# The up-projection of a streaming encoder: all tiles take unnormalised rows, root and shift are applied in PSUM

## The reference

```python
def rms_norm(x, g):
    y = xf * lax.rsqrt(jnp.mean(xf * xf, axis=-1, keepdims=True) + EPS)
    return (y * g)

def conv_ffn(h, w_up, w_conv, b_conv, w_down, prefix):
    up = h @ w_up                                   # 1024 -> 2 * 2816
    ext = jnp.concatenate([prefix, up], axis=1)     # 2 earlier rows
    conv = ext[:, 0:T] * w_conv[0]
    for j in range(1, CONV_W):                      # CONV_W = 3
        conv = conv + ext[:, j:j + T] * w_conv[j]
    conv = conv + b_conv
    gate, val = jnp.split(conv, 2, axis=-1)
    return (jax.nn.silu(gate) * val) @ w_down, ext[:, T:]

    # in a layer, x after the token mixers:
    h = rms_norm(x, g2) * (1 + scale2) + shift2
    f, conv_state = conv_ffn(h, w_up, w_conv, b_conv, w_down, conv_prefix)
    x = x + gate2 * f
```

## Time and profile before

| | us |
|---|---|
| median of 3 runs | 1171.86 |
| lowest and highest of them | 1171.85, 1176.35 |
| the profiled execution, its own time | 1171.43 |
| the span in its trace | 1169.7 |
| what lies around the span | 1.7 |

### The profile page before, as it was taken

How to read it: one execution, slowest core, us unless ns; L and a number is a source line. 1 busy time by engine, 2 the same in 40 slices (tenths; PEclk the granted TensorE clock), 3 DMA queues, 4 the chain that set the end, 5 groups by cost and what they waited for, 6 DMA issues and landing times.

```text
span 1169.7 us, 22931 instructions
## 1 busy us (share of the span) xinstructions
PE 1119.6 (96%) x8368; PEld 1017.8 (87%) x8368; DVE 515.3 (44%) x1297; ACT 591.3 (51%) x1095; POOL 691.8 (59%) x310
## 2 busy tenths in 40 slices
PE   5799999999999899999999999999999999999996
PEld 1687888887889899999998788888889989999996
DVE  0556513546325754442136562355631575444102
ACT  1454444445445666555456544445544566555431
POOL 0454434545455687778778544454556668777782
PEclk8899999999999999999999999999999999999999
DMA  9855546755553355454456555483534325545451
GB/s 361 299 178 207 221 187 237 257 205 195 195 199 111 106 180 170 153 179 158 171 200 237 204 217 197 181 305 119 198 109 140 124 98 180 179 147 177 144 189 71
DMA packets 61821, 215.99 MB, mean 185 GB/s; under 512 B 7896, under 2 KB 8480, under 8 KB 61488
## 3 DMA queue, kind: packets, MB, share of 16 engines
q1 hardware_dynamic: 61744, 214.92, 51.6%
HBM read 209.85 MB, written 5.05 MB: 184 GB/s over the span
## 4 chain that ended last, share of the span: by engine, by line
PE 86%; DVE 6%; POOL 2%; issue 2%; ACT 2%; DMA 1%; SPq 1%; DVEq 0%; POOLq 0%; ACTq 0%
PE ps L637 25%; PE ps L638 23%; PE ps L639 23%; PE ps L590 4%; PE ps L606 2%; POOL wlo L535 1%; PE ps L584 1%; DMA first<-mod_first 1%; POOL hl L553 1%; DVE ps L1758 1%; PE ps L798 1%; DVE merged L1766 1%; PE ps L764 1%; PE ps L674 1%; PE ps L754 1%
## 5 line engine op out<-in xcount | busy, mean ns | idle before, releaser
L535 POOL TENSOR_TENSOR wlo<-raw,whi 128x1024 fp32r<-128x1024 f32 x282 | 673.5, 2392 | 450.4 <-ACT whi L1109 348.2
L637 PE MATMUL ps<-hh,whi 128*128 128x288 f32 (+1 forms) x1648 | 501.4, 304 | 15.2 <-POOL wlo L535 3.6
L638 PE MATMUL ps<-hl,whi 128*128 128x288 f32 (+1 forms) x1648 | 489.6, 297 | 0.0
L639 PE MATMUL ps<-hh,wlo 128*128 128x288 f32 (+1 forms) x1648 | 489.0, 297 | 0.0
L637 PEld LDWEIGHTS ps<-hh,whi 128*128 128x128 f32 x1648 | 312.3, 190 | 55.9 <-issue 37.7
L638 PEld LDWEIGHTS ps<-hl,whi 128*128 128x128 f32 x1648 | 313.1, 190 | 0.6
L639 PEld LDWEIGHTS ps<-hh,wlo 128*128 128x128 f32 x1648 | 312.1, 189 | 0.0
L1109 ACT ACTIVATE whi<-raw 128x1024 fp32r<-128x1024 f32 x204 | 214.6, 1054 | 139.3 <-PE ps L639 108.6
L637 PE MATMUL ps<-fah,whi 128*128 128x290 f32 x352 | 107.4, 305 | 0.0
L638 PE MATMUL ps<-fal,whi 128*128 128x290 f32 x352 | 104.5, 297 | 0.0
L639 PE MATMUL ps<-fah,wlo 128*128 128x290 f32 x352 | 104.4, 297 | 0.0
(11 more groups left out here) (234 smaller groups left out, 1232.4 us busy)
## 6 DMA issues: line engine op xcount, KB each, us to landing
raw<-stream SPq DMA_DIRECT2D x284, 512.0 KB, 4.4
mraw<-stream SPq DMA_DIRECT2D x40, 1024.0 KB
first<-mod_first SPq DMA_DIRECT2D x16, 512.0 KB, 10.7
o_proj<-proj SPq DMA_DIRECT2D x12, 288.0 KB
kvk<-keys_t SPq DMA_DIRECT2D x6, 512.0 KB, 3.8
kvv<-vals SPq DMA_DIRECT2D x6, 512.0 KB, 5.1
cst<-consts SPq DMA_DIRECT2D x1, 1238.0 KB, 17.3
x<-x_fm SPq DMA_DIRECT2D x1, 1152.0 KB, 11.8
```

The costliest lines, as they stand in the source:

```text
L535: nc.gpsimd.tensor_tensor(wlo[:, slot, :], raw[:, slot, :], whi[:, slot, :].bitcast(F32), ALU.subtract).then_inc(lo_ready, 1)
L637: mm(out, whi[:, slot, a:b], high, start=(i == 0 and wcols[2]), stop=False)
L638: mm(out, whi[:, slot, a:b], low, start=False, stop=False)
L639: last = mm(out, wlo[:, slot, a:b], high, start=False, stop=(i == n - 1 and wcols[3]))
```

## The change

All 44 up tiles of a layer now take `oh` and `ol`. `scale_tile` and `shift_up` are applied to each of them, and `up_shifted` takes the place of `piece_done` ahead of the copy of the state. `hup` and everything that made the normalised rows of this stage is gone on DVE, ACT and POOL. PE's tiles 4 and 5, too, now wait for the convolution of tiles 0 and 1 (the loop covers them). The split of piece Q_UP + 4 on ACT is moved ahead of the load of the table for silu, and inside `up_pair` the split of a piece stands ahead of the shift.

```diff
@@ PE
-                for j in range(4):
-                    up_piece(slot_for(l, Q_UP + j), Q_UP + 4 + j, UPB + j, j + 1 if j >= 2 else None, hl_ready if j == 0 else None)
-                with pe.Fori(0, 2 * FT // 4 - 2) as r:
+                with pe.Fori(0, 2 * FT // 4 - 1) as r:
                     for j in range(4):
-                        up_piece(slot_for(l, Q_UP + j), r * 4 + (Q_UP + 8 + j), UPB + j, r * 4 + (j + 5))
+                        pe.wait_ge(lo_ready, upto(l, lo_ready, r * 4 + (Q_UP + 4 + j + 1)))
+                        pe.wait_ge(convolved, upto(l, convolved, r * 4 + (j + 1)))
+                        product(ps[:, UPB + j, 2:2 + CC], slot_for(l, Q_UP + j), (1, 0, True, True), u_terms).then_inc(piece_done, 1)
@@ POOL
-                lows(q, Q_UP + AHEAD)
-                q = lows_and_norm(Q_UP + AHEAD, 2, ((1, 0, 2), (1, 2, 5), (1, 5, KT)))
                 lows(q, NSPLIT + (AHEAD if l + 1 < DEPTH else 0))
@@ ACT
                 high(Q_UP + AHEAD)
                 root(2)
+                high(Q_UP + AHEAD + 1)
                 nc.scalar.preload_act_table_set("silu_and_others")
...
-                for j in range(3):
-                    shift_up(j)
-                    if j < 2:
-                        high(Q_UP + AHEAD + 1 + j)
-                    norm_high(2, *UP_CHUNKS[j])
...
                 def up_pair(p, odd, r=None):
-                    up_tile(p, odd, 0, r)
-                    if r is None and p == 0:
-                        shift_up(3)
+                    next_high(p, odd, 0, r)
+                    shift_up(p, odd, 0)
                     if r is not None or p >= 1:
                         silu(p - 1, 1 - odd)
-                    up_tile(p, odd, 1, r)
+                    up_tile(p, odd, 0, r)
+                    next_high(p, odd, 1, r)
+                    shift_up(p, odd, 1)
                     if r is not None or p >= 1:
                         product_high(p - 1, 1 - odd)
+                    up_tile(p, odd, 1, r)
@@ DVE
-                for j in range(3):
-                    scale_tile(Q_UP + j, up_bank(j), 2, None)
-                    if j == 0:
-                        in_order(V.tensor_copy(ps[:, 7, 0:T], rstd[:]))
-                    normed(2, *UP_CHUNKS[j])
+
+                def scale_up(p, odd, g):
+                    u = 2 * odd + g
+                    dve.wait_ge(piece_done, upto(l, piece_done, p * 2 + (done(Q_UP) + g)))
+                    V.tensor_copy(shifts[:, u, :], ps[:, up_bank(p, u), GAP:GAP + 2])
+                    scale_tile(up_bank(p, u), 2, up_scaled)
...
                 def pair(p, odd, first=False):
-                    convolve(p, odd, 0)
+                    scale_up(p, odd, 0)
                     if not first:
                         multiply(p - 1, 1 - odd)
-                    convolve(p, odd, 1)
+                    convolve(p, odd, 0)
+                    scale_up(p, odd, 1)
                     if not first:
                         product_low(p - 1, 1 - odd)
-
-                convolve(0, 0, 0)
-                scale_tile(Q_UP + 3, up_bank(3), 2, None)
-                convolve(0, 0, 1)
+                    convolve(p, odd, 1)
+
+                pair(0, 0, True)
                 pair(1, 1)
```

More of the change, by code:

```diff
@@ L130 @@
 AHEAD = 3
-NI, NU = 6, 4
+NI = 6
 C_ID, C_ONE = 0, P
@@ L209, in encoder @@
         fal, _, n2 = place("fal", [P, FT, CC], F32R, at=proj_at + n)
-        hup, _, n3 = place("hup", [P, KT, CC], F32, at=proj_at + n + n2)
-        assert n + n2 + n3 <= gates_at + gates_n - proj_at and n + n2 >= proj_n
+        assert n + n2 <= gates_at + gates_n - proj_at
         probs, _, n = place("probs", [P, 1024], F32, at=work_at)
@@ L546, in lows, with norm_low @@
                         low(slot_for(l, q), q)
[L548 to L550 removed]
+                def norm_low(a, b):
                     for k in range(a, b):
[L552 to L553 removed]
+                        pool.wait_ge(hh_ready, upto(l, hh_ready, k + 1))
+                        nc.gpsimd.tensor_tensor(hl[:, k, :], work[:, k, :], hh[:, k, :].bitcast(F32),
                                                 ALU.subtract).then_inc(hl_ready, 1)
[L557 to L564 removed]
                 if l == 0:
@@ L570, in _ @@
                 else:
-                    q = lows_and_norm(Q_IN + AHEAD, 1, ((3, 0, 1), (1, 1, 4), (1, 4, KT)))
-                lows(q, Q_UP + AHEAD)
-                q = lows_and_norm(Q_UP + AHEAD, 2, ((1, 0, 2), (1, 2, 5), (1, 5, KT)))
+                    q = Q_IN + AHEAD
+                    for pieces, a, b in ((3, 0, 1), (1, 1, 4), (1, 4, KT)):
+                        lows(q, q + pieces)
+                        q += pieces
+                        norm_low(a, b)
+                        pool.sem_inc(settled, 1)
                 lows(q, NSPLIT + (AHEAD if l + 1 < DEPTH else 0))
@@ L1031, in _ @@
                         sum_square(l, 2, m - 1)
-                def up_piece(slot, q, bank, convolved_tiles, ready=None):
-                    pe.wait_ge(lo_ready, upto(l, lo_ready, q + 1))
-                    if convolved_tiles is not None:
-                        pe.wait_ge(convolved, upto(l, convolved, convolved_tiles))
-                    product(ps[:, bank, 2:2 + CC], slot, (1, 0, True, True), up_terms, ready, KT).then_inc(piece_done, 1)
-                for j in range(NU):
+                for j in range(4):
                     pe.wait_ge(lo_ready, upto(l, lo_ready, Q_UP + j + 1))
-                    o = ps[:, up_bank(j), 2:2 + CC]
                     if j == 0:
                         pe.wait_ge(pads_ready, upto(l, pads_ready, 1))
+                    o = ps[:, up_bank(j // 2, j), 2:2 + CC]
+                    if j == 0:
                         i = first_tile(o, slot_for(l, Q_UP), 2)
@@ L1548, in in_order, with affine, normed @@
                     dve.wait_ge(dve_own, count[0] + at)
-                def affine(n, k, scaled):
+                def affine(k, scaled):
                     for g, (a, b) in enumerate(((0, TP), (TP, T))):
-                        o = work[:, k, a:b] if n == 1 else hup[:, k, a + 2 * g:b + 2 * g]
-                        i = V.tensor_scalar(o, scaled[:, a:b], norm_a[:, n - 1, k, g:g + 1],
-                                            mod[:, 24 * (n - 1) + k, g:g + 1], ALU.mult, ALU.add)
+                        i = V.tensor_scalar(work[:, k, a:b], scaled[:, a:b], norm_a[:, 0, k, g:g + 1], mod[:, k, g:g + 1],
+                                            ALU.mult, ALU.add)
                     i.then_inc(h_scaled, 1)
-                def normed(n, a, b):
-                    half = [ps[:, bank, 2:2 + T] for bank in (6, 2 if n == 1 else 1)]
-                    at = (n - 1) * KT
+                def normed(a, b):
+                    half = [ps[:, bank, 0:T] for bank in (6, 2)]
                     for k in range(a, b + 1):
@@ L1611, in _ @@
                         dve.wait_ge(x_scaled, upto(l, x_scaled, k + 1))
-                        affine(1, k, work[:, k, :])
+                        affine(k, work[:, k, :])
                         if k:
@@ L1620, in _ @@
                     for t in range(NI):
-                        scale_tile(t, t % 2, 0, cst[:, C_QS + t:C_QS + t + 1])
+                        dve.wait_ge(piece_done, upto(l, piece_done, done(t)))
+                        V.tensor_scalar(shifts[:, t, :], ps[:, t % 2, TP:TP + 2], cst[:, C_QS + t:C_QS + t + 1], None, ALU.mult)
+                        scale_tile(t % 2, 0, in_scaled)
                         if t == 0:
                             in_order(V.tensor_copy(ps[:, 7, 0:T], rstd[:]))
-                        normed(1, *IN_CHUNKS[t])
+                        normed(*IN_CHUNKS[t])
                 def rotate(n):
```

90 lines of the change are left out of this document (34 added, 56 removed).

## The result

| | before | changed |
|---|---|---|
| median of 4 runs each, us | 1173.17 | 1259.48 |
| lowest and highest, us | 1171.85, 1176.35 | 1257.11, 1262.44 |
| the profiled execution, us | 1171.43 | 1257.11 |
| its span, us | 1169.7 | 1255.0 |

The changed kernel takes 1.0733 times as long, with a 95% interval of 1.0695 to 1.0770. The forecast was 1254.5 us, range 1238 to 1275.

What follows compares the result with a forecast made beforehand. The prediction took the turns of DVE and ACT as the bound: 2.61 + 1.69 = 4.30 us a tile against PE's 3.22. That added 2 x 41.4 = 82.8 us to 1171.43, forecast 1254.5 us, range 1238 to 1275.

Steps and rivals of the forecast that it cites:

- What bounds the kernel: Up-stage loop: DVE and ACT work in turns, 2.61 us from state copy to state copy, under PE's 3.22 us tile.
- Removal: Transition into the up stage: dropping normalised rows saves at most 5.2 us a layer, 10.4 us in all, if PE stays bound.
- The turn, 4.30 us: Up-stage loop: 2.61 us plus 1.69 us for scaling, shift, silu or product_high, hand-overs and register steps, against PE's 3.22 us.
- the register step: Loop, between some waits and their instruction: adds 0.08 us a turn on average, with 0 and 0.2 us as ends.
- The start: Layer 0's up stage: first scaling at 387.25 as before, first shift at 388.7, tile 4 scaled at 402.0.
- What comes back: End of the up stage: last tap to last product shortens by 0.3 us; down stage moves by 41.4 us a layer.
- The split: ACT, behind the tail: splitting a weight piece costs nothing, with 0.9 us of cover before the next shift.
- what would show it: Timeline signs: state copies 4.2 to 4.4 us apart, PE idle about 1 us before each up tile, chain over DVE and ACT.
- PE stays the bound: Rival, up loop: scaling and shift overlap the previous tile's convolution, turn under 3.22 us; 1161 us, chance 0.06.
- Silu off the path: Rival, up loop: silu and product_high stay outside the turn, 3.88 us a turn; 1221 us, chance 0.03.
- PE's clock: Rival, up loop: waits lower PE's granted clock until PE is the bound; above 1275 us, chance 0.05.

Runs made afterwards that it cites:

- the open ring: Against the changed kernel: scaling and shift issued one tile ahead, weight pieces split four ahead and before the shift, nothing left out; 1161.22 us, 0.9897 of before.
- the rows alone: Against the changed kernel: unnormalised rows for all up tiles, but scaling and shift left out and the earlier kernel's order kept; 1160.73 us, 0.9891 of before.
- the half low half: Against the changed kernel: POOL forms only 512 of 1024 columns of `wlo` for pieces 4 to 43; 1261.69 us in one run.
- the kernel one tile ahead: Against the changed kernel: same work, DVE scales and ACT shifts tile n+1 during tile n, shift ahead of the next split; 1240.48 us, 1.0578 of before.

## Why the prediction was right

**What bounds the kernel.** Right. The turn of DVE and ACT, read from its waits and not from busy shares, was the quantity to follow. The experiment without silu in the turn and the one without the shift each moved the time by what they moved of the turn (0.26 us a tile and 19 us in the one, 0.41 us a tile and 36 us in the other), and with both steps hidden the open ring was back at PE's pace.

**Removal.** I took 10.4 us as the most. The kernel with the rows alone gained 10.8 us by its profiled execution and 12 to 13 by the medians: right in size, a little low. In the changed kernel none of it is seen, since PE no longer sets the pace.

**The turn, 4.30 us.** Measured 4.344 us. Scaling 0.59, hand-over 0.03 and shift 0.54 stand in the rows above as put. The term that was a little too small is the register step, put at 0.08 us on average: silu takes 0.42 and the multiplication starts 0.56 us after silu, so 0.14 us for what the prediction gave 0.11, and the third tap starts 0.40 and 0.33 us after the copies at 452.21 and 456.61, where it gave 0.35. At the end of the stage, outside the loop, the last product waited 0.48 us for 0.41 us of product_high. It is 0.04 us a turn, 0.04 x 39 = 1.7 us a layer.

**The start.** The first shift was put at 388.7 and came 0.2 us later; tile 4 was put at 402.0:

```profile
402.33 0.15 DVE L1920 COPY shifts<-ps 128x2 f32<-128x2 f32 x1
...
575.71 0.52 DVE L1936 SCALAR_TENSOR_TENSOR conv<-ps,vec,conv 128x290 f32<-128x290 f32 x1
```

The last tap of layer 0 ends at 576.23, put at 574.1. Against the earlier trace rows that is 43.8 us later, not 41.7 us: 0.3 us from the start, 1.7 us from the turns, and 0.1 us in the last tile. In layer 1 it is 43.4 us, put at 41.6.

**What comes back, and two terms that weren't in the sum.** The prediction let the start of the down stage move with the last product, less 0.3 us. From the last tap to the last product it is 0.2 us less (1.57 us from start to start, 1.74 us before), so the product is 43.6 us late. But it isn't what PE waited for before. The third piece of the first down tile (7 terms, 21 matmuls) is the one that needs it. Its first matmul, and the first of the next down tile, in the kernel before:

```profile
535.85 0.29 PE L637 MATMUL ps<-fah,whi 128*128 128x290 f32 x1
...
538.73 0.37 PE L637 MATMUL ps<-fah,whi 128*128 128x290 f32 x1
```

and in the changed kernel:

```profile
577.88 0.58 PE L627 MATMUL ps<-fah,whi 128*128 128x290 f32 x1 [2.34 <-DVE fal L1946]
...
582.35 0.37 PE L627 MATMUL ps<-fah,whi 128*128 128x290 f32 x1
```

Before, the last product ended at 534.12, 1.7 us ahead of its use, and PE didn't wait. Now PE waits, and the third piece starts 42.0 us late and not 43.6. That is 1.6 us in favour of the changed kernel. Then its 21 matmuls take 4.47 us for 2.88, because PE's granted clock fell in the wait (the last section has it). That is 1.6 us against it, and the next down tile starts 43.6 us late. In layer 1 the two are 1.5 us (the third piece starts 84.1 us late, the last product 85.6) and 1.6 us (4.42 us for 2.86). The prediction had neither term. That they cancel is luck; with the slack alone the sum would have been some 3 us lower.

One more gift wasn't in the sum. Early in layer 1's token mixers ACT waits for a transfer, in the kernel before (first row) and in the changed one (second row):

```profile
624.02 1.06 ACT L1109 ACTIVATE whi<-raw 128x1024 fp32r<-128x1024 f32 x1 [3.46 <-DMA raw<-stream]
```

```profile
666.30 1.06 ACT L1093 ACTIVATE whi<-raw 128x1024 fp32r<-128x1024 f32 x1 [2.46 <-DMA raw<-stream]
```

Ahead of this wait the changed kernel is 43.3 us behind, after it 42.3 us. What released ACT was a transfer, and that was less late than ACT. The ends add up: 43.8 to the last tap of layer 0, 42.3 at the first scaling of layer 1, another 43.4 in its up stage, 0.5 back at the end (0.4 of it in layer 1's down projection, whose tiles are 0.05 us shorter; the cause of that is open), 85.3 us in all, where 82.8 was put. The forecast lies 5.0 us under the median: 2.9 us of it are this sum (1257.11 us for 1254.2), and the rest is that the profiled execution was the fastest of four, which go up to 1262.44 us.

**The split.** That it costs nothing was right, and the half low half shows it for POOL too. But one detail of "what would show it" was wrong: it had PE's idle time released by DVE's second instruction of the convolution. It is released by POOL's low half, because the split of a piece stands in ACT's queue behind the tail of each tile and so comes once a turn, and split and low half (1.1 and 2.4 us) end after the convolution that also lets PE go. The term cost nothing, so the sum didn't suffer. It did cost the expectation of the kernel one tile ahead, where the same path became the bound.

**The rivals.** *PE stays the bound* would have been true with another order: the open ring took 1161.22 us, and the rival said 1161. The Trainium skill (Perfetto Trace Analysis, Identifying the Most-Contended Engine) has the engine with the highest occupancy as the one to relieve first. Before, that was PE, and the run with the rows alone agrees: taking PE's waits away, by itself, gave 12 to 13 us. But from the low shares of DVE and ACT, 44% and 51%, it doesn't follow that they had room for the work that this relief needed: with it the kernel took 7.3% longer. *Silu off the path* said 3.88 us a turn and 1221 us; with silu taken off by hand it was 4.09 us and 1240.83 us, mostly for the two waits named above. *PE's clock* did not come in the loop: the granted clock is 1.00 from 408 to 530 us, with an idle time of about 0.9 us in each 4.34 us. It fell at the end of the up stage and cost the 1.6 us a layer named above.

## What to carry to other kernels

Before work is moved to an engine with room, find out whether it waits in turns with another: if each of two engines waits once per tile for the other, add the steps from start to start around one turn, put each new step in at its place, and compare with the tile time of the bound. If the turn gets too long, issue the new steps one tile ahead, into the waits that are there already. Then follow the second ring, through the slots of the input (here split, low half, matmuls): a step that waits for the bound engine must stand behind whatever feeds that engine, not ahead of it.

## What the runs showed of the hardware

The granted clock of PE fell in the two long waits at the end of the up stage, and not in the many short ones of the loop. In the timeline of PE of the changed kernel, the first two matmuls of the down projection (the second wait is at 577.88 in the rows further up):

```profile
567.90 0.58 PE L627 MATMUL ps<-fah,whi 128*128 128x290 f32 x1 [3.37 <-DVE conv L1936]
568.28 0.45 PE L628 MATMUL ps<-fal,whi 128*128 128x290 f32 x1
```

The first whole window of 2 us after each of the two waits:

```profile
568.00:570.00 2.00, 2.00 (x9) 2.00 (x10) 0.64 (x4) 1.12 (x4) 1.67 (x1) 0.50 0.00 0
...
578.00:580.00 2.00, 2.00 (x9) 2.00 (x10) 0.00 (x0) 1.99 (x4) 0.20 (x1) 0.50 0.00 0
```

After waits of 3.37 and 2.34 us the matmuls ran at 0.50, which is 1.2 GHz, and took 0.45 us instead of 0.30. The first fall cost nothing, since PE waited again for the last product. The second cost 1.6 us, since nothing waited behind it: the 21 matmuls of the third piece are the path there. In layer 1 a wait of 2.23 us in the same place did the same. The waits of 0.75 to 0.94 us ahead of the three tiles from 452.39 to 461.14 in the loop left the clock at 2.4 GHz. The Trainium skill (TensorE: Matmul & The Clock Gate, A second HAM failure mode: psum-queue depth-cycling) tells of short idle times that make the clock go down and up; the loop here, with an idle time ahead of every tile, doesn't show it.

A wait for an instruction of the same engine costs, too, in the kernel with silu out of the turn: 0.55 us from the first tap to a multiplication that waits for it, 0.44 us to a step that doesn't.
